# Two key heads from one 128-column projection in the windowed attention layer

## What is computed

```python
B_HEADS, B_KV_HEADS, B_HDIM, B_WINDOW = 16, 4, 64, 128
q, k, v, gate = jnp.split(h @ w_in, [B_WIDTH, B_WIDTH + B_KVW, B_WIDTH + 2 * B_KVW], axis=-1)
q_x = apply_rope_2(q_x, cos, sin)      # only the 512 sequence tokens are rotated
k_x = apply_rope_2(k_x, cos, sin)
s_band = where(abs(qpos - kpos) <= B_WINDOW, q_x . k_x * scale, NEG_INF)
s_ctx  = q_x . k_c * scale             # context queries: s_cc = q_c . k_c * scale
p = softmax([s_ctx, s_band, sink])
y = ((p @ v) * silu(gate)) @ w_out
```

## Time and profile before

| | |
|---|---|
| Median of three runs | 3069.0 us (3064.4 to 3070.97) |
| Span of the profiled execution, first to last instruction | 3058.8 us |
| TensorE busy | 2886.6 us, 94% of the span |
| VectorE busy | 1816.5 us, 59% |
| ScalarE busy | 1157.1 us, 38% |
| Mean granted TensorE clock | 0.984 |
| Windowed attention, first row maximum to the end of tile 7 | about 1593 to 1900 us of the span |

### The profile page before, as it was taken

How to read it: one execution, slowest core, us unless ns; L and a number is a source line. 1 busy time by engine, 2 the same in 40 slices (tenths; PEclk the granted TensorE clock), 3 DMA queues, 4 the chain that set the end, 5 groups by cost and what they waited for, 6 DMA issues and landing times.

```text
span 3058.8 us, 36212 instructions
## 1 busy us (share of the span) xinstructions
PE 2886.6 (94%) x14485; PEld 2322.3 (76%) x14485; DVE 1816.5 (59%) x3295; ACT 1157.1 (38%) x2054; POOL 93.8 (3%) x177
## 2 busy tenths in 40 slices
PE   7999999999999999999999888999998988999997
PEld 5777767778888787887797776788875656777885
DVE  6546568877675566663646667465435767445553
ACT  4234343232223434444524445443222212553443
POOL 0000000100000000000100000020000000000000
PEclk9999999999999999999999999999999998999999
DMA  6322116645453331103211111333331211221102
GB/s 242 102 90 91 65 64 216 247 146 180 158 179 117 104 131 62 59 25 104 83 54 29 32 32 38 113 110 106 101 91 51 63 54 60 104 69 54 39 18 97
DMA packets 109314, 288.79 MB, mean 94 GB/s; under 512 B 18326, under 2 KB 37815, under 8 KB 108888
## 3 DMA queue, kind: packets, MB, share of 16 engines
q1 hardware_dynamic: 97880, 249.05, 24.7%
q0 software_dynamic: 9392, 32.48, 2.9%
q10 hardware_dynamic: 1872, 4.93, 0.4%
HBM read 257.05 MB, written 24.12 MB: 92 GB/s over the span
## 4 chain that ended last, share of the span: by engine, by line
PE 83%; DVE 9%; ACT 6%; issue 1%; DMA 0%; SPq 0%; ACTq 0%; POOL 0%; DVEq 0%; POOLq 0%
PE ps L1884 20%; PE ps L1886 20%; PE ps L1885 20%; PE ps L2132 4%; PE ps L2197 2%; PE ps L2171 2%; PE ps L1917 2%; PE ps L2213 2%; PE ps L2119 2%; ACT pt L2469 2%; PE ps L2160 1%; PE ps L2033 1%; PE ps L2087 1%; PE ps L2089 1%; ACT tmp L2464 1%
## 5 line engine op out<-in xcount | busy, mean ns | idle before, releaser
L1884 PE MATMUL ps<-hh,whi 128*128 128x256 f32 (+1 forms) x2424 | 915.2, 378 | 32.5 <-DVE hl L2651 12.9
L1885 PE MATMUL ps<-hl,whi 128*128 128x256 f32 (+1 forms) x2424 | 870.4, 359 | 0.0
L1886 PE MATMUL ps<-hh,wlo 128*128 128x256 f32 (+1 forms) x2424 | 870.3, 359 | 0.0
L1884 PEld LDWEIGHTS ps<-hh,whi 128*128 128x128 f32 x2424 | 458.8, 189 | 137.3 <-issue 31.6
L1885 PEld LDWEIGHTS ps<-hl,whi 128*128 128x128 f32 x2424 | 460.3, 190 | 88.2 <-issue 19.3
L1886 PEld LDWEIGHTS ps<-hh,wlo 128*128 128x128 f32 x2424 | 458.6, 189 | 71.0
L2660 DVE TENSOR_TENSOR wlo<-raw,whi 128x1024 fp32r<-128x1024 f32 x249 | 303.9, 1222 | 234.0 <-ACT whi L2276 233.7
L2276 ACT ACTIVATE whi<-raw 128x1024 fp32r<-128x1024 f32 x249 | 262.4, 1055 | 292.5 <-PE ps L1886 247.5
L2132 PE MATMUL ps<-pt,v 128*128 128x256 f32 x768 | 205.2, 388 | 18.1 <-ACT pt L2469 18.1
L2469 ACT ACTIVATE pt<-ps 128x512 f32<-128x512 f32 (+1 forms) x200 | 109.0, 578 | 223.9 <-PE ps L2119 223.5
L2993 DVE TENSOR_REDUCE sm<-ps 128x1 f32<-128x768 f32 (+3 forms) x176 | 129.5, 736 | 98.6 <-PE ps L2089 48.9
(11 more groups left out here) (379 smaller groups left out, 4516.2 us busy)
## 6 DMA issues: line engine op xcount, KB each, us to landing
raw<-in_wall SPq DMA_DIRECT2D x249, 512.0 KB, 4.2
mb<-in_wmod SPq DMA_DIRECT2D x128, 512.0 KB, 3.6
xb<-xpark SPq DMA_DIRECT2D x24, 384.0 KB, 4.6
xpark<-F POOLq DMA_DIRECT2D x32, 256.0 KB, 2.3
upark<-tmp POOLq DMA_DIRECT2D x18, 384.0 KB, 2.8
u<-upark SPq DMA_DIRECT2D x24, 256.0 KB, 2.9
tmp<-tmp SPq DMA_DIRECT2D x80, 64.0 KB, 2.0
early<-in_wm SPq DMA_DIRECT2D x8, 512.0 KB, 6.8
```

What stands on the lines that cost most here:

```text
L1884: e.matmul(out, L[0], R[0], start=start, stop=False)
L1885: e.matmul(out, L[0], R[1], start=False, stop=False)
L1886: return e.matmul(out, L[1], R[0], start=False, stop=stop)
```

## The change

Two key heads are now projected from one 128-column weight tile that holds the 64 columns of the one and the 64 columns of the other (`("keys", 172, 178)` and `("keys", 181, 186)`, each loaded by two DMAs in pieces of 64 columns from the two doubled tiles in memory). `make_k` is called twice, `make_k(0)` ahead of the loop and `make_k(1)` in tile 2, where `make_k(2)` stood; the calls in tiles 0 and 4 are gone. The product has head A on rows 0 to 63 and head B on rows 64 to 127. So each head is written to both row halves of its buffer by copies and subtractions of 64 rows, four of each for a token group (`pair`, `pair_lo`), where one of 128 rows stood for each head. The key buffers have three places, since two heads are made at once while one is in use.

```diff
-    KG = [sb([P, 2, T], F32R, "kg", sS) for _ in range(2)]
+    KG = [sb([P, 3, T], F32R, "kg", sS) for _ in range(2)]
-    ..., 172, 173, ("values", 174, 182), ("values", 175, 183),
-             178, 176, 177, 181, 179, 180, 186, 184, 185, 187, ...
+    ..., ("keys", 172, 178), 173, ("values", 174, 182), ("values", 175, 183),
+             176, 177, ("keys", 181, 186), 179, 180, 184, 185, 187, ...
-        kb, qb = Ring(2), Ring(2)
+        kb, qb = Ring(3), Ring(2)
-        def make_k(n):
+        def make_k(pair):
             def evac(g):
-                p = kb.take()
-                b2["kg", n] = p
-                dst = [KG[x][:, p.i, :] for x in range(2)]
+                p = [kb.take() for _ in range(2)]
+                b2["kg", 2 * pair], b2["kg", 2 * pair + 1] = p
                 for i, (a, b) in enumerate(g.groups):
+                    bank = g.banks[i]
+                    dst = [[KG[x][:, q.i, a:b] for q in p] for x in range(2)]
                     if a == NC_:
-                        rope_stages(g, i, CS2, (s_cs2, "cs2"), None, SW32, dst[0][:, a:b], dst[1][:, a:b], ("kg", l, n), (p, free), att.later)
+                        name = ("kg", l, pair)
+                        j, m = tmps.take(), tmps.take()
+                        stage("rope", g, bank, ps[:, bank.i, 0:NX], CS2, (s_cs2, "cs2"), None, SW32, j, m, name)
+                        banks.drop(bank)
+                        def turn(): stage("rope_add", NX, CS2, j, m, name); tmps.drop(j)
+                        def high(): stage("pair", None, TMP[:, m.i, 0:NX], dst[0], name, (p, free))
+                        def low(): stage("pair_lo", TMP[:, m.i, 0:NX], *dst, name, m); tmps.drop(m)
+                        for n, f in enumerate((turn, high, low)):
+                            att.later(f, n)
                     else:
-                        stage("split", ...)
+                        stage("pair", g, ps[:, bank.i, 0:NC_], dst[0], ("kgc", l, pair), (p, free))
+                        stage("pair_lo", ps[:, bank.i, 0:NC_], *dst, ("kgc", l, pair), bank)
...
-                    if qt == 2 and tile % 2 == 0 and tile < 6:
-                        make_k(tile // 2 + 1)
+                    if qt == 2 and tile == 2:
+                        make_k(1)
...
+        def pair(g, src, dst, name, free):                 # ScalarE
+            wait_all(w, (pe, g) if g else (dve, ("roped", name)), free)
+            for s in range(2):
+                for half in range(2):
+                    x = A(dst[s][64 * half:64 * half + 64, :], src[64 * s:64 * s + 64, :], ACT.Copy)
+            x.then_inc(*act.up(name))
...
+        def pair_lo(src, hi, lo, name, b):                 # VectorE
+            w.wait_ge(*act.of(name))
+            for s in range(2):
+                rows = slice(64 * s, 64 * s + 64)
+                for half in range(2):
+                    x = TT(lo[s][64 * half:64 * half + 64, :], src[rows, :], hi[s][rows, :].bitcast(F32), ALU.subtract)
+            x.then_inc(*dve.up(name, b))
...
+            if s[0] == "keys":                             # SyncE, parts of a weight tile
+                new = out.rearrange("p (k i c) -> p k i c", i=2, c=64)
+                return [(new[:, :, i, :], wall[s[1 + i]].rearrange("p (k c) -> p k c", c=P)[:, :, 0:64]) for i in range(2)]
```

More of the change, by code:

```diff
@@ L287, in latent_tiles @@
         return [("list", base, tuple(x[i:i + 8])) for i in range(0, 80, 8)]
-    tiles = [*range(33), 34, 35, 33, *range(36, 146), *latent_tiles(146), *range(156, 172), 172, 173, ("values", 174, 182), ("values", 175, 183),
-             178, 176, 177, 181, 179, 180, 186, 184, 185, 187, *range(188, 220), *(("blocks", 220, x) for x in (0, 8, 16)), ("long", 0), *(("blocks", 220, x) for x in (28, 40, 56)), ("long", 1),
+    tiles = [*range(33), 34, 35, 33, *range(36, 146), *latent_tiles(146), *range(156, 172), ("keys", 172, 178), 173, ("values", 174, 182), ("values", 175, 183),
+             176, 177, ("keys", 181, 186), 179, 180, 184, 185, 187, *range(188, 220), *(("blocks", 220, x) for x in (0, 8, 16)), ("long", 0), *(("blocks", 220, x) for x in (28, 40, 56)), ("long", 1),
              *(("blocks", 220, x) for x in (64, 80))]
@@ L2093, in score @@
                 w.wait_ge(*dve.of(("q2c", l, h)))
-                w.wait_ge(*dve.of(("kg", l, u["grp"])))
-                w.wait_ge(*dve.of(("kgc", l, u["grp"])))
+                w.wait_ge(*dve.of(("kg", l, u["grp"] // 2)))
+                w.wait_ge(*dve.of(("kgc", l, u["grp"] // 2)))
                 q = u["q"][:, s, qt * P:qt * P + P]
@@ L2562, in scalar_program @@
               "merge_split": merge_split, "ffn_gate": ffn_gate, "ffn_split": ffn_split, "setup2": setup2, "cq": cq, "rope_raw": rope_raw,
-              "raw_copy": raw_copy, "silu": silu, "half": half, "exp": exp, "turn": turn, "stack": stack, "v_twice": v_twice, "o_split": o_split, "out_take": out_take,
+              "raw_copy": raw_copy, "silu": silu, "half": half, "exp": exp, "turn": turn, "stack": stack, "pair": pair, "v_twice": v_twice, "o_split": o_split, "out_take": out_take,
               "sine": sine, "net_split": net_split, "conv3": conv3, "filter": filter_, "kf": kf, "tables_fill": tables_fill, "z_turn": z_turn, "conv_out": conv_out}
@@ L3146, in vector_program @@
               "coef_in": coef_in, "coef_out": coef_out, "o_split": o_split, "out_square": out_square, "out_add": out_add, "rope_raw": rope_raw,
-              "latent": latent, "silu": silu, "half": half, "score": score, "bias": bias, "weights_of": weights_of, "stack_lo": stack_lo, "take": take,
+              "latent": latent, "silu": silu, "half": half, "score": score, "bias": bias, "weights_of": weights_of, "stack_lo": stack_lo, "pair_lo": pair_lo, "take": take,
               "sine": sine, "conv3": conv3, "filter": filter_, "kf": kf, "fw_in": fw_in, "fold": fold,
```

11 lines of the change are left out of this document (9 added, 2 removed).

## The result

The changed kernel takes 3055.97 us (median of 20 runs, 3049.56 to 3064.45), the kernel before 3068.61 (20 runs, 3057.1 to 3071.3). The ratio of the runs is 0.9971, with a 95% interval of 0.9961 to 0.9981: about 9 us less (6 to 12), where the medians are 12.6 apart. It is faster, and more likely than not by over 0.2%, but the interval reaches to 0.19%. The forecast was 3055.4 us and a ratio of 0.9956. The time was met; the gain was forecast too large, just outside the interval.

A forecast was written before the change was run, and what follows sets the result against it. TensorE was taken as the bound, busy 94% of the span, with waits inside the windowed attention; -11.8 - 5.0 + 3.2 = -13.6 us takes 3069.0 to 3055.4 us, own range 3051 to 3059, overall range 3050 to 3062.

The forecast's parts named there:

- Tile 4, -11.8 us: Tile 4 loses its key projection with nothing in its place and goes from 47.7 to 35.9 us, 11.8 less.
- Tile 0 with the start-up, -5.0 us: Tile 0 loses its key projection while the start-up ahead of it grows; together 5.0 us less.
- the ceiling: Upper bound for tile 0 with the start-up: 6.8 us less, block 3's scores waiting only for the first exponentials.
- Tile 2, +3.2 us: Tile 2 projects a pair instead of one head; a longer wait and more VectorE subtractions cost 3.2 us.
- The 2.05 us of the low part: In tile 2, VectorE's four rotated subtractions stand ahead of the normalising product and add 2.05 us to the path.
- The wait for `take`: In tile 2, make_q(3) waits for `take` 4.3 us instead of 3.2, a cost of 1.15 us.
- a cost I had called covered: In tile 2, context subtractions hold the next transposition's bank about 1.1 us longer, covered by the longer wait behind it.
- The clock: the step that failed: In tile 4, the 3.3 us stretch at clock 0.50 goes with the wait before it: 11.8 us gained, not 10.2.
- the rival: Clock falls in new pauses of tiles 0 and 2: two stretches of 1.6 us, 10.5 us gained, 3058.5 us; chance 0.17.
- stretches in tiles 0 to 2: Sign against the prediction: it is wrong if the clock shows stretches of 0.50 in tiles 0 to 2.
- The base: The runs' median lies 10.2 us above the profiled span of 3058.8; carried over, so the forecast starts from 3069.0 us.
- The transfer of the gain to the end: Behind the layer the order stays the same, so the whole gain reaches the end; time behind 1900 us changes at most 2 us.

The follow-up runs named there:

- the version with this edit alone: The kernel before without the key projection make_k(3) in tile 4, all else kept; ratio 0.9973 to the kernel before.
- early and filled version: The changed kernel with the pair's three rotation stages moved behind `take` and matmuls on zeros in pauses of tiles 0, 1, 3 to 7; ratio 0.9934 to before.
- writes of whole rows: The changed kernel with the pair's writes made by one 128-row instruction per head, high and low, half as many instructions; ratio 0.9957 to the kernel before.
- interleaved start-up: The early and filled version with key and query stages ahead of tile 0 interleaved: both rotations, both high parts, both low parts; ratio 0.9934 to the kernel before.
- early low part: The changed kernel with the four rotated low-part subtractions one gap earlier, at the end of block 3's step; ratio 0.9962 to the kernel before.
- filled version: The changed kernel with matmuls on zeros ahead of block 3's scores (all tiles but 2) and of make_q(3); ratio 0.9935 to the kernel before.

## Why the prediction came out as it did

*Tile 4, -11.8 us: right for the tile.* 47.7 became 36.0 in the version with this edit alone, where a stretch in tile 7 took 1.6 us back. In the changed kernel it became 37.3, by a stretch of its own. The choice of 11.8 over 10.2 belongs to the clock, below.

*Tile 0 with the start-up, -5.0 us: right, and 0.9 of it lost to the clock.* Without the pair's writes tile 0 gives 6.5, near the ceiling. The start-up grew by 2.5 us to the first row maximum (forecast 2.3). The scores of block 3 began 30.4 us behind the first write of a key for 35.9, 5.5 us earlier; so much lies between the prediction's own times for them too (1597.6 and 1603.07), where its text says 5.2. `make_q(1)` began 35.3 us behind that write for 39.5, only 4.2 us earlier, since 3.3 of the 4.9 us between the two ran at 0.50. With the clock at 1.00, in the early and filled version, it began at 34.3, 5.2 us earlier. The writes of whole rows and the interleaved start-up each bring the first row maximum back to 25.9, which ties the delay to the chain of the pair's writes.

*Tile 2, +3.2 us: right within 0.3.* 49.6 for 46.1 where the clock stays up. The 2.05 us of the low part were shown by the early low part (2.1 back). The wait for `take` was 3.2 us and not 4.3: the rotation did start later, but the bank of the transposition, held by the context subtractions (1.0 us, a cost I had called covered), moved the value products behind it too, so the wait itself didn't grow. The sum of both is what was forecast.

*The clock: the step that failed.* "I take 11.8, because the stretch follows the wait that goes" counted one stretch less and none more; the rival had two. There were five and six, also behind pauses of 1.4 us. The prediction had named stretches in tiles 0 to 2 as a sign that it is wrong, and they stood in tiles 0 and 2. It called the waits besides `take` short handshakes of at most 0.9 us, while the same view had the five waits of up to 1.4 us shown above. In tiles 1, 3, 5 and 6 of before they had left no mark. Filling the pauses took every stretch away, in three traces of three, and gave 4.6 to 6.2 us back in the layer's window. That is the missing part: 13.6 forecast, 11.4 in the window of the filled version, 6.8 and 5.2 in the two traces of the changed kernel. Of the last 2.2 us, 1.5 are the start-up's and tile 0's, where with the fill a transposition waits 1.3 us for the normalising product that it doesn't wait for without (1.1 us in the early and filled version); 0.3 are tile 2's, and the rest is a tenth in each of four tiles.

The Trainium skill, "TensorE: Matmul & The Clock Gate" (Why this matters for your kernels), advises against idle gaps between bursts of matmuls. The rival that went with it had a chance of 0.17; its 10.5 us less is a ratio of 0.9966, inside the measured interval, so it was weighed too lightly. The trace agrees with the page in tiles 0 and 2 (pauses of 2.8 and 3.2 us), and the one of before doesn't in its tile 2 (3.2 us, and a clock of 1.00). The page speaks of longer gaps than the 1.4 us of tiles 3 to 6, where most of the stretches stood.

*What stays open.* Why a pause brings the lower clock in one tile and not in another. Tiles 3 to 6 ran at 1.00 in the version without tile 4's projection and tile 7 did not, behind the same pause; tiles 3 to 5 had the lower clock in the changed kernel. The traces of the filled versions show that the pauses are needed for it, not what else is.

*The base.* The 10.2 us laid between span and median were not around the span: 1.8 us are, and the other 8.4 came from a profiled execution shorter than the median run. Carrying the difference over was harmless for the median, by luck: the medians are 12.6 us apart, where the ratio gives 9. The ratio times the base of 3069.0 is 3060.1 us, which lies outside 3051 to 3059, the forecast's own range.

*The transfer of the gain to the end* can't be told from the spans. What follows tile 7's first row maximum took 1185.5 us in both first traces, and 1180.4 in the changed kernel's second.

## What to carry to other kernels

Compare what a piece of work costs where it stands with what it would cost well placed, before taking it away: the key projections of tiles 2 and 4 cost 10 to 12 us in their place, for 8.3 us of matmuls, and 6.8 us once the rotation no longer stood in front of the instruction that frees a bank. In an in-order queue, a stage that waits for a DMA goes behind everything that someone waits for. Work taken out of TensorE can bring the lower clock to pauses that it left as they were, so the granted clock of the tiles that weren't touched belongs in the comparison; zero matmuls in the pauses are a cheap test.

## What the runs showed of the hardware

Stretches of 0.50 in the granted clock (1.2 GHz for 2.4) lasted 3.4 us, twice 6.8 us. One of 3.4 us lengthened an attention tile (3 to 6) by 1.0 to 1.6 us and tile 2 or 4 by 1.5 to 1.6 where it lay in projection matmuls. They came in or behind pauses of 3.2, 2.8 and 1.4 us, and not with every one of 3.2 and 1.4. ScalarE and VectorE instructions of 64 rows took as long as those of 128 (379 and 384 ns, 631 and 632, 422 and 424, 686 and 692). Up to the first write of a key, where the edits have done next to nothing, thirteen traces differ by 11.7 us, and behind tile 7's first row maximum by 7.0, of which 1.6 us are the stretch in tile 7 of one of them. Two executions of the changed kernel differ by 2.9 and 5.1 us there. The change is worth about 9 us; only a window cut around the edit makes two traces comparable.
